# Norms of a two-layer diffusion backbone: roots with tokens on partitions, products on three engines, router on four column strips, and a value product by halves

## The reference

```python
def rms_norm(x, g):
    y = xf * lax.rsqrt(jnp.mean(xf * xf, axis=-1, keepdims=True) + RMS_EPS)
    return y * g

def run_layer(x, mod, l, P, rope, ctx):
    shift1, scale1, gate1, shift2, scale2, gate2 = jnp.split(mod, 6, axis=-1)
    h = rms_norm(x, P['norm1_g'][l]) * (1 + scale1) + shift1
    y, new = even_mixer(...) if l % 2 == 0 else odd_mixer(...)     # layer 0: LRU and differential attention
    x = x + gate1 * y
    h = rms_norm(x, P['norm2_g'][l]) * (1 + scale2) + shift2
    x = x + gate2 * expert_choice_ffn(h, P['router_w'][l], ...)    # softmax(h @ router_w), top 80 per expert, 16 experts

def diff_attention_block(qb, k, v, lam):
    s = jnp.einsum('bqhcd,bkhcd->bhcqk', qb, k) * HEAD_DIM ** -0.5
    p = jax.nn.softmax(s, axis=-1)
    a = p[:, :, 0] - lam * p[:, :, 1]
    return jnp.einsum('bhqk,bkhe->bqhe', a, v)
```

## Time and profile before

| | us |
|---|---|
| median of three runs (lowest, highest) | 1799.83 (1792.06, 1801.79) |
| the profiled execution | 1796.14 |
| its span, first to last instruction | 1794.2 |
| TensorE busy | 1606.8 |
| VectorE, ScalarE, GpSimd busy | 645.0, 441.5, 239.6 |

### The profile page before, as it was taken

How to read it: one execution, slowest core, us unless ns; L and a number is a source line. 1 busy time by engine, 2 the same in 40 slices (tenths; PEclk the granted TensorE clock), 3 DMA queues, 4 the chain that set the end, 5 groups by cost and what they waited for, 6 DMA issues and landing times.

```text
span 1794.2 us, 37806 instructions
## 1 busy us (share of the span) xinstructions
PE 1606.8 (90%) x16674; PEld 1031.5 (57%) x16674; DVE 645.0 (36%) x1300; ACT 441.5 (25%) x744; POOL 239.6 (13%) x237
## 2 busy tenths in 40 slices
PE   5999975998949999998999989988889959999992
PEld 2554433664526776764555558667675537776761
DVE  5234466562270000003129636634462270000003
ACT  4111175451031111112110246432231032111100
POOL 0000000000001111100000026156540001111103
PEclk8999997898979999999999999999999989999996
DMA  9832281235127999996112100011115127999994
GB/s 345 295 122 94 100 292 43 94 123 206 50 103 275 376 379 381 384 392 195 47 53 89 50 1 1 1 49 50 49 50 199 65 88 264 372 384 381 384 395 138
DMA packets 90318, 330.07 MB, mean 184 GB/s; under 512 B 10708, under 2 KB 16456, under 8 KB 82024
## 3 DMA queue, kind: packets, MB, share of 16 engines
q1 hardware_dynamic: 76016, 287.29, 42.1%
q0 software_dynamic: 9168, 32.65, 6.6%
q10 hardware_dynamic: 5032, 8.65, 1.3%
HBM read 303.79 MB, written 24.78 MB: 183 GB/s over the span
## 4 chain that ended last, share of the span: by engine, by line
PE 82%; DVE 9%; DMA 3%; ACT 3%; issue 2%; ACTq 0%; POOL 0%; DVEq 0%
PE pairs L222 27%; PE pairs L1342 16%; PE pairs L1354 12%; PE pairs L1051 2%; PE pairs L1325 2%; PE pairs L1065 1%; PE pairs L341 1%; PE pairs L1811 1%; PE pairs L1831 1%; PE pairs L1794 1%; PE pairs L2038 1%; PE pairs L486 1%; PE pairs L2049 1%; PE pairs L1179 1%; DMA ring<-in_w_in_ab 1%
## 5 line engine op out<-in xcount | busy, mean ns | idle before, releaser
L222 PE MATMUL pairs<-hT,ring 128*128 128x128 f32 (+1 forms) x1120 | 306.2, 436 | 2.2 <-ACT hT L355 2.2
L222 PEld LDWEIGHTS pairs<-hT,ring 128*128 128x128 f32 x1120 | 170.3, 192 | 139.0 <-issue 139.0
L355 ACT ACTIVATE arena<-pairs 128x512 f32<-128x512 f32 (+6 forms) x208 | 120.9, 600 | 423.2 <-PE pairs L222 201.6
L222 PE MATMUL pairs<-ring,hT 128*128 128x512 f32 (+1 forms) x448 | 177.4, 557 | 0.0
L1342 PEld LDWEIGHTS pairs<-arena,ring 128*64 128x64 f32 x4096 | 143.1, 137 | 15.9 <-issue 15.9
L1342 PEld LDWEIGHTS pairs<-arena 128*64 128x64 f32 x4096 | 142.9, 137 | 13.8 <-issue 13.7
L1342 PE MATMUL pairs<-arena,ring 128*64 128x80 f32 x4096 | 146.3, 233 | 2.4 <-issue 2.4
L1342 PE MATMUL pairs<-arena 128*64 128x80 f32 x4096 | 145.8, 233 | 2.0 <-ACT arena L1377 1.0
L222 PEld LDWEIGHTS pairs<-ring,hT 128*128 128x128 f32 x448 | 84.8, 190 | 92.1 <-issue 89.1
L1410 DVE TENSOR_SCALAR hT<-pairs,arena 80x512 f32<-80x512 f32 x32 | 23.9, 747 | 272.0 <-ACT hT L1386 272.0
L1354 PE MATMUL pairs<-ring,arena 128*80 128x512 f32 x256 | 112.7, 593 | 0.2 <-DMA ring<-in_exp_w 0.2
(11 more groups left out here) (386 smaller groups left out, 2150.3 us busy)
## 6 DMA issues: line engine op xcount, KB each, us to landing
arena<-in_exp_w SPq DMA_DIRECT2D x48, 2048.0 KB, 18.3
ring<-in_exp_w SPq DMA_DIRECT2D x48, 2048.0 KB, 20.1
ring<-in_w_mod SPq DMA_DIRECT2D x24, 2048.0 KB, 8.2
ring<-in_w_in_ab SPq DMA_DIRECT2D x5, 2048.0 KB, 11.6
ring<-in_w_in_cd SPq DMA_DIRECT2D x5, 2048.0 KB, 7.8
ring<-in_w_out SPq DMA_DIRECT2D x4, 2048.0 KB, 7.7
moe_rows<-arena POOLq DMA_DIRECT2D x2, 2560.0 KB, 14.5
h_rows<-arena POOLq DMA_DIRECT2D x2, 2560.0 KB, 8.4
```

Of the source, the lines that this page charges most:

```text
L222: last = pe.matmul(out, lhs(k), rhs(k), start=(k == 0), stop=(k == KD - 1))
L355: return eng.activation(dst, src, ACT.Copy) if eng is nc.scalar else eng.tensor_copy(dst, src)
```

## The change

- **Norm.** The column sums come with tokens on partitions: five products of 128 tokens each with one column of ones. Root and reciprocal are taken on 128x5 (`root5`). VectorE spreads the five columns over a diagonal (`diag5`), TensorE multiplies it by ones (`norm_spread_pe`, two products), ScalarE copies the result into `rstd` (`norm_spread_act`).
- **Products.** x times `rstd` is a product of whole 640-column tiles: tiles 0, 1, 3, 4, 6 on VectorE, 2, 5, 7 on GpSimd (`norm_pool`, new in GpSimd's order at four places). Scale and shift are one instruction per group of tokens: tiles 0, 1, 2, 3, 5 on ScalarE, 4, 6, 7 on VectorE.
- **Router.** The weights are zero-padded to 32 columns; tile k goes to partitions 32 (k mod 4) to 32 (k mod 4) + 31, and the turn into rows becomes a product with `strips`, which adds the four strips. An exponential on one column is put ahead of the copies. SyncE's queue waits for the zeroing before it loads the router's weights.
- **Attention.** The value product is done in two halves of 64 partitions: the upper half ahead of `scores(i, 0)`, the lower behind `scores(i, 1)`.
- **Fill products.** Six become two ahead of the layer-1 projection and the routers; new are three and two in the attention's first two rounds and three ahead of `dy_turn`.

```diff
@@ norm_pe
-            pe.matmul(ps[:, 0:NS], ones, ssum[:, 0:NS], start=True, stop=True)
-            finish(pe.matmul(ps[:, NS:T], ones, ssum[:, NS:T], start=True, stop=True), u)
+            for t in range(NT):
+                last = pe.matmul(ps[:, t:t + 1], ssum[:, t * P:t * P + P], ones[:, 0:1], start=True, stop=True)
+            finish(last, u)
+        def norm_spread_pe(pe, l, n):
+            pe.wait_ge(S("n_diag"), 2 * l + n + 1)
+            pe.matmul(ps[:, 0:NS], ones, diag5[:, 0:NS], start=True, stop=True)
+            finish(pe.matmul(ps[:, NS:T], ones, diag5[:, NS:T], start=True, stop=True), u)
+        X_DVE, X_POOL = (0, 1, 3, 4, 6), (2, 5, 7)
+        H_ACT, H_DVE = (0, 1, 2, 3, 5), (4, 6, 7)
+        def norm_pool(g, l, n):
+            emptied(g, ("nrb", l, n))
+            for k in X_POOL:
+                g.tensor_tensor(hT[:, k, :], xT[:, k, :], rstd, ALU.mult).then_inc(S("x_pool"), 1)
@@ norm_rstd_dve
-            step(v.reciprocal(rstd, rstd))
+            step(v.reciprocal(root5, root5))
+            v.tensor_tensor(diag5.rearrange("p (t c) -> p t c", c=P), ident.unsqueeze(1).broadcast_to((P, NT, P)),
+                            root5.unsqueeze(2).broadcast_to((P, NT, P)), ALU.mult).then_inc(S("n_diag"), 1)
@@ norm_scale_dve
-                    v.scalar_tensor_tensor(out=hT[:, k, a:b], in0=xT[:, k, a:b], scalar=gsc[:, l, n, k, g:g + 1],
-                                           in1=rstd[:, a:b], op0=ALU.mult, op1=ALU.mult)
+            for k in X_DVE:
+                v.tensor_tensor(hT[:, k, :], xT[:, k, :], rstd, ALU.mult).then_inc(S("x_dve"), 1)
+                if k in H_DVE:
+                    shifted(k)
+            shifted(7)
@@ rows (diff_pe)
+                r = slice(64 - 64 * half, 128 - 64 * half)
+                if half == 0:
+                    take(pe, u, 3)
+                    emptied(pe, ("daT", i))
+                else:
+                    pe.wait_ge(S("d_half"), i + 1)
...
+                    last = pe.matmul(PSUM[:, 3, 0:P], aT[i % 2][r, j * P:j * P + P], vals[r], start=(half == j == 0),
+                                     stop=(half == 1 and j == nk - 1))
@@ the rounds
+                if 0 <= i - 3 < len(ITS):
+                    rows(i - 3, 0)
                 if i < len(ITS):
                     scores(i, 0)
                 if 0 <= i - 2 < len(ITS):
                     turn(i - 2)
+                if i < 2:
+                    keep_busy(pe, PSUM[:, 2, :], 3 if i == 0 else 2)
...
                 if 0 <= i - 3 < len(ITS):
-                    rows(i - 3)
+                    rows(i - 3, 1)
...
             pe.wait_ge(bank_free[7], banks.uses[7])
+            keep_busy(pe, bank_of(7), 3)
@@ route_pe
-            keep_busy(pe, ps, 6)
+            keep_busy(pe, ps, 2)
+                out = ps[32 * (k % 4):32 * (k % 4) + 32, :]
+                pe.matmul(out[:, 0:NS], wr[:, l, k, :], hT[:, k, 0:NS], start=(k < 4), stop=(k >= 4))
...
-                        last = pe.transpose(ps[:, NE * j:NE * j + NE], affT[:, j * P:j * P + P], ident[0:NE, 0:NE])
+                        last = pe.matmul(ps[:, NE * j:NE * j + NE], logits4[:, j * P:j * P + P], strips[:, :],
+                                         start=True, stop=True)
@@ route_act
+            act.activation(sps[:, 6:7], sps[:, 0:1], ACT.Exp)
```

More of the change, by code:

```diff
@@ L113, in build @@
         sdel = sb("sdel", [P, 8, P])
-        wr = sb("wr", [P, 2, KD, NE])
+        wr = sb("wr", [P, 2, KD, 32])
+        strips = sb("strips", [P, NE])
         sm = sb("sm", [P, 640])
@@ L404, in setup_dve @@
             release(v.tensor_copy(cA[:, :], ps[:, 0:P]), "cols")
+            v.tensor_reduce(strips[:, :], ident.rearrange("p (q r) -> p r q", r=32)[:, 0:NE, :], AX_X, ALU.add)
             flip_in_read(v, "x_in", 1)
@@ L589, in norm_root_act @@
             ps = filled(act, ("nrm", l, n))
-            release(act.activation(rstd, ps[:, 0:T], ACT.Sqrt, scale=1.0 / D, bias=1e-6), ("nrm", l, n))
+            release(act.activation(root5, ps[:, 0:NT], ACT.Sqrt, scale=1.0 / D, bias=1e-6), ("nrm", l, n))
         def norm_shift_act(act, l, n):
-            i = 2 * l + n
-            for k in range(KD):
+            for k in H_ACT:
+                normed(act, l, n, k)
                 for g in range(2):
                     a, b = seg[g]
-                    act.wait_ge(S("h_scaled"), i * 16 + 2 * k + g + 1)
-                    act.activation(hT[:, k, a:b], hT[:, k, a:b], ACT.Identity,
-                                   bias=modt[:, l, 24 * n + k, g:g + 1]).then_inc(S("h_ready"), 1)
+                    ins = act.activation(hT[:, k, a:b], hT[:, k, a:b], ACT.Identity, scale=gsc[:, l, n, k, g:g + 1],
+                                         bias=modt[:, l, 24 * n + k, g:g + 1])
+                ins.then_inc(S("h_act"), 1)
         def norm_add(v, l, n, k):
@@ L1054, in scores, with rows @@
                     finish(pe.matmul(ps[:, 0:P], q, k[:, T:768], start=True, stop=True), u)
-            def rows(i):
+            def rows(i, half):
                 t, h = ITS[i]
@@ L1059, in rows @@
                 u = ("do", i)
-                ps = take(pe, u, 3)
-                emptied(pe, ("daT", i))
+                r = slice(64 - 64 * half, 128 - 64 * half)
+                if half == 0:
+                    take(pe, u, 3)
+                    emptied(pe, ("daT", i))
+                else:
+                    pe.wait_ge(S("d_half"), i + 1)
                 for j in range(nk):
@@ L1064, in rows @@
                         dv_c[:, h * P:h * P + P] if j == 0 else vr[:, j - 1, h * P:h * P + P]
-                    last = pe.matmul(ps[:, 0:P], aT[i % 2][:, j * P:j * P + P], vals, start=(j == 0), stop=(j == nk - 1))
-                finish(last, u)
+                    last = pe.matmul(PSUM[:, 3, 0:P], aT[i % 2][r, j * P:j * P + P], vals[r], start=(half == j == 0),
+                                     stop=(half == 1 and j == nk - 1))
+                if half == 1:
+                    finish(last, u)
+                else:
+                    last.then_inc(S("d_half"), 1)
             def dy_turn(t):
@@ L1161, in build @@
         lg = ar(18700, NT, NE)
-        affT = ar(18800, T)[0:NE, :]
+        logits4 = ar(18800, T)
+        affT = logits4[0:NE, :]
         g16 = ar(19500, CAP)[0:NE, :]
@@ L1175, in route_pe @@
             ps = take(pe, u)
-            keep_busy(pe, ps, 6)
+            keep_busy(pe, ps, 2)
             for k in range(KD):
-                pe.wait_ge(S("h_ready"), 16 * (2 * l + 1) + 2 * k + 2)
-                pe.matmul(ps[0:NE, 0:NS], wr[:, l, k, :], hT[:, k, 0:NS], start=(k == 0), stop=(k == KD - 1))
-                last = pe.matmul(ps[0:NE, NS:T], wr[:, l, k, :], hT[:, k, NS:T], start=(k == 0), stop=(k == KD - 1))
+                h_here(pe, l, 1, k)
+                out = ps[32 * (k % 4):32 * (k % 4) + 32, :]
+                pe.matmul(out[:, 0:NS], wr[:, l, k, :], hT[:, k, 0:NS], start=(k < 4), stop=(k >= 4))
+                last = pe.matmul(out[:, NS:T], wr[:, l, k, :], hT[:, k, NS:T], start=(k < 4), stop=(k >= 4))
             finish(last, u)
@@ L1527, in sum_pe @@
                     pe.wait_ge(S("sq"), 16 + j + 1)
-                    for a, b in seg:
-                        last = pe.matmul(acc[:, a:b], ones, sq_all[:, j, a:b], start=(j == 0), stop=(j == KD - 1))
+                    for t in range(NT):
+                        last = pe.matmul(acc[:, t:t + 1], sq_all[:, j, t * P:t * P + P], ones[:, 0:1],
+                                         start=(j == t == 0), stop=(j == KD - 1 and t == NT - 1))
             finish(last, un)
@@ L2591, in _ @@
                 if l == 0:
-                    for i in range(2, 4):
-                        mod_act(act, i)
+                    mod_act(act, 2)
+                norm_spread_act(act, l, 0)
+                if l == 0:
+                    mod_act(act, 3)
                 norm_shift_act(act, l, 0)
@@ L2688, in _ @@
             setup_pool(g)
+            norm_pool(g, 0, 0)
             layer0_outputs(g)
+            norm_pool(g, 0, 1)
             route_pool(g, 0)
             moe_pool(g, 0)
+            norm_pool(g, 1, 0)
             layer1_outputs(g)
```

47 lines of the change are left out of this document (39 added, 8 removed).

## The result

| | before | changed |
|---|---|---|
| median time, us (lowest, highest) | 1797.94 (1792.06, 1801.79) | 1825.20 (1820.74, 1839.07) |
| ratio (95% interval) | | 1.017 (1.010 to 1.023) |
| profiled execution, its span | 1796.14, 1794.2 | 1828.03, 1826.1 |
| mean granted TensorE clock | 0.953 | 0.944 |

The account below looks back on a forecast made before the run. TensorE bounds the kernel, holding 82% of the chain. Savings of 4.8 (attention loop), 1.2 (its tail), 1.2 at each router, 1.4 (norm before layer 1) and 0 (first norm) sum to 9.8 us: 1790, range 1778 to 1804.

Parts of the forecast that it names:

- The ring: Attention: the half ahead of the scores waits for the accumulator that VectorE frees; a closed loop of 4.59 us per item.
- Score start to VectorE 1.45: Attention, first term of the 4.59 us loop: 1.45 us from the scores' start to VectorE.
- The trade of 20.2 for 20.5 per four items: Attention, regular stretches: four items with the halves take 20.2 us instead of 20.5.
- third rival: Attention: halves do not hide beside scores; 1818, or 1800 if eight records can be passed; chance 0.13, half of it at 1800.
- second rival: TensorE's clock falls in the attention's loop and the norms' gaps; items about 7.9 us, 10 more, 1800; chance 0.22.
- Start: Attention's first rounds: fill products close the table-load gap and its low clock; item 4 at 17.0 instead of 24.3, 7.3 won.
- last four: Attention, items 13 to 15: two halves of 1.3 beside scores of 0.4; 2 us lost.
- tail: Attention's end: three fill products ahead of the five last turns; 1.2 us won, between 1 lost and 3 won.
- Lock: Norms: VectorE's and GpSimd's products lock each other out; tile 7 ready 10.4 us after the root's copy.
- the sums cost the same (ten records, 1.0, for 1.07): Norm before layer 1: column sums by one-column products take 1.0 us where they took 1.07.
- the 1.4: Norm before layer 1: first projection product 1.4 us earlier after the sums, 0 if GpSimd gets the first turn.
- The table load's 1.28: Routers: an early exponential takes ScalarE's 1.28 us table load off the softmax's wait.

Follow-up runs that it names:

- e10_ring_filled: Changed kernel with one fill product behind the lower half in rounds 3 to 15; 1822.0 us, 1.013 to 1.019 of the kernel before.
- e1_whole: Changed kernel with the value product whole again, over 128 partitions at the end of each round; 1807.4 us, 1.005 to 1.010 of the kernel before.
- e3_all_dve: Changed kernel with all eight products by the root on VectorE, none on GpSimd; 1819.9 us, 1.012 to 1.019 of the kernel before.
- e5_order: Changed kernel with the probabilities' turn behind the third of five row tiles at both routers; 1825.5 us, 1.014 to 1.020 of the kernel before.

## Why the prediction was wrong, point by point

**The ring.** The mechanism was named and its sum had one wrong term. "Score start to VectorE 1.45" was kept as it was, as if the scores started with the half; they started 0.77 after it, and 1.45 then passed exactly. With the other terms as forecast the ring is 4.59 + 0.77, within 0.02 of the 5.34 in the rows. The trade of 20.2 for 20.5 per four items became 22.9. This was the mild form of the third rival ("if eight records can be passed, the first scores start 0.65 late"), to which I gave half of 0.13. I priced it at 10 for sixteen items; at full clock the twelve rounds of the table would take 3 x 22.9 = 68.7, 8 more than the 60.7 of before. The Trainium skill, "TensorE: Matmul & The Clock Gate", section "The mechanism", says that matmuls keep their order in start and end. The trace differs: the first score record (341.20) starts before the half's last three (341.31), so TensorE does not always start products in the order in which they are written. But seven of ten started first, and that is the cost.

**The clock.** The second rival, at 0.22, said that an item costs 7.9 at the low level and that there are three falls of an item or so each. Measured: 8.9 an item, two falls of 17 us each; they cost 83.5 - 68.7 = 15 us. The forecast held 2. Beside the 0.77 left out of the ring, the failed step is taking the rivals one at a time: the longer ring makes the idle time in which the clock falls (filled in e10_ring_filled, it does not fall). Together they are the 23 us lost in these rounds, and no case of mine had both in full.

**Start, last four, tail.** Won 5.8 in the first four rounds (7.3 forecast); last four rounds 2.1 lost (2 forecast); tail, from the last scaling to the output projection, 10.2 to 9.8, and some of the 2.3 behind it (0.3 to 2.3 in the other kernels with these fills): with 1.2 forecast, right in sign.

**Lock.** Right for the products at the routers: VectorE's take 2.1 beside GpSimd's, and tile 7 is ready 10.3 after the copy (10.4 forecast). That the logits came at 16.62 for 16.5 is in part luck. In five other kernels with the same norm and router code they come at 17.7 at layer 0, later than before, because the spread's two products take 2.5 us at a clock of 0.50 (e1_whole); in the changed kernel's trace they took 1.4 at 0.88. So the 0.6 won at layer 0 hangs on the clock, which the sum had at its full level. In the first norm the steps on the gain lose 2.3 us by GpSimd's products (e3_all_dve shows the rows without them), and the first product another 1.35. That is 3.7 of the 4.7 lost where the forecast had 0, with 0.5 lost as its bound. I had applied the lock to the products only. The Trainium skill, "SBUF — State Buffer", section "Who interferes with whom", speaks of any VectorE instruction with two SBUF inputs, and the step of 1.49 beside GpSimd's first product agrees with it. The step of 1.17 starts ahead of that product's record, beside a transfer that holds up nothing in e3_all_dve; how the products hold it up, no run shows.

**Norm ahead of layer 1.** "the sums cost the same (ten records, 1.0, for 1.07)" was right for the first tiles, 1.17, and wrong at the low level, 2.13: 6.9 us lost in the sums. The price of a product was taken from four of them in a row at full clock, and not asked for forty. The first product: GpSimd's first turn took the 1.4 away, as the bound said, and the spread at the low clock took another 1.2.

**Routers.** The strips' turn cost 0.8 (0.7 forecast). The table load's 1.28 was counted as won because the softmax waited for it; but behind the softmax stands TensorE's queue. The trace of before had the rows:
```profile
512.42 3.71 PE L1186 MATMUL pairs<-cst,hT 128*128 128x128 f32 x32
...
515.25 0.24 DVE L1270 TENSOR_TENSOR arena<-arena,sm 128x80 f32<-128x80 f32 x1
...
515.97 0.71 PE L1200 MATMUL pairs<-cst,arena 128*16 128x128 f32 x5
```
The probabilities, ready at 515.49, are turned (L1200) only when the row turns are at their end: I had not asked what would be late next. e5_order shows it. From the logits' copy to the top tokens it is now 7.13 us for 6.47 before, 0.7 lost where 0.6 was to be won. (With the logits of the other five kernels the router takes 24.8 or 24.9 us, not 23.8.)

## What to carry to other kernels

When a product is moved ahead of another in one engine's queue, its wait and its length go with it: sum the ring with the moved piece in it, and ask what the clock does in the idle time of that ring. Put the piece that waits behind the one that feeds the other engine; in this kernel that order alone was 20 us. Where a wait is taken away, look in the trace at what the next instruction's own engine still has queued.

## What the runs showed of the hardware

Two products on different halves of the rows take 1.39 us together when the long score product is issued first (343.17 to 344.56), 2.1 when the ten short records are first (340.43 to 342.55). TensorE can be busy for 100% of a stretch and stand at 0.50 of its clock: it did in 11 us of mostly one-column products, and not when these had 128 columns. With GpSimd's products behind them, VectorE's instructions of 8 and 16 columns took 1.0 and 1.3 us longer than without; only the second lies beside a product in the trace.
